# A hybrid streaming encoder on one core: other step sizes for the state-space scans, and ninety matmuls fewer at the end

## The chip, the cores and the metric

The kernel runs on one core of a Trainium2 chip. The metric is the device time of one execution in microseconds (us). TensorE is called PE below, its weight load PEld, VectorE DVE, ScalarE ACT, GpSimd POOL and SyncE SP.

## What is computed

One inference step of an encoder with two layers, for 512 new prompt frames and 64 sample frames, width 1024. Layer one mixes by an S5 state-space recurrence, layer two by differential attention over shared keys and values. Both have a SwiGLU feed-forward block before and after the mixer, and a LayerNorm behind each. All in fp32. The part that the change touches is the recurrence:

```python
bu_re = bu_re.at[:, 0].add(lb_re * h_re - lb_im * h_im)
bu_im = bu_im.at[:, 0].add(lb_re * h_im + lb_im * h_re)
_, _, hs_re, hs_im = lax.associative_scan(complex_affine_combine, (a_r, a_i, bu_re, bu_im), axis=1)
y_blk = jnp.einsum('gcp,btgp->btgc', c_re, hs_re) - jnp.einsum('gcp,btgp->btgc', c_im, hs_im)
```

It is an exact regrouping of a linear recurrence, h(t) = lambda h(t-1) + B u(t), with complex lambda.

## The kernel before, in words

The 576 frames are worked on in two halves: half 0 has 256 columns, half 1 has 320. The weights are cut into tiles of 128 output channels by 7 or 8 rows of 128 inputs. SP loads tile n (`raw`, four buffers), ACT casts it to its high part (`wh`, L509), DVE subtracts that from it for the low part (`wl`, L515), and PE makes three matmuls for each row of it (L537 to L539). There are three buffers of `wh` and `wl`, so the cast of tile n+3 waits until PE is through with tile n (`tile_done`), then comes `wl`, and PE may start tile n+3. DVE also takes the products out of PSUM: L675 (`hf`) in the first product of a feed-forward block, L698 (`r`) in the second.

All engines run programs in order, written out by hand. Work that goes beside the weight tiles is a Python generator; behind each weight tile the code calls `step(beside)`, which issues the work up to the next `yield`. What stands between two `yield`s therefore stands between two `wl` subtractions in DVE's queue. The same count of steps is kept on PE, ACT and POOL, so that the parts meet.

The S5 scans are such side work. `dve_scan` (L1519 on) runs once per half `h` and group `grp` of channels, four times in all: half 0 beside the feed-forward block of half 1, half 1 beside the first block of the next stage, which works on half 0. A scan goes up `LEVELS` = 4 levels and down again. Each call of `advance` is five DVE operations: L1533 (`sa`, a product over m elements a partition), L1535 and L1537 (`sb`, two products of m/2), L1539 and L1542 or L1544 (two additions of m into `hs`). `link` makes the next operation wait for the one before. For half 0 m is 1024, 512, 256 and 128 on the way up, for half 1 it is 1280, 640, 320 and 160; then three or four short calls (m = 32, and 64 in half 1), a few copies, and the levels in reverse order.

`packed(work, room)` divides a scan into steps: each operation yields a size, and a step ends once the sizes have come to `room` (the excess is carried on). The size of an operation is its m plus 60. `SCAN_ROOM` is 1800 for half 0 and 1620 for half 1. `paced(..., SCAN[h])` gives a scan 11 steps in half 0 and 15 in half 1. By these sizes the division (the copies counted as one operation) in half 0 has 3, 2, 3, 4, 10, 17, 7, 5, 2, 2 and 1 operations in its steps, in half 1 it has 2, 2, 1, 2, 3, 5, 10, 17, 7, 4, 3, 1, 2, 2 and 0.

When a scan has ended (its last addition, L1544, raises `s_sh`), PE takes its states in matmuls with the output tables (L1728 and L1731 in `pe_s5`). In PE's program these stand at a fixed step: two steps behind the scan's last one, by the same count. DVE and ACT then copy the results (`ysb`, L1496), ACT takes their gelu (L1653).

At the very end the last rows of the result are transposed (L2529), normalised on DVE (L2569, L2575) and stored by SP (L2591); SP then waits for the stores to land. Behind its last transpose PE has 90 more matmuls (L2923, the loop over `FILL`), which write a PSUM bank that nobody reads.

Of the kernel before, what the change touches and what calls it, by code (L numbers as in the profile page):

```python
# [15 lines left out]
P = 128  # L16
# [72 lines left out]
def _ffn(f, h, held=False):  # L89

    for p in range(len(PARTS)):
# [37 lines left out]
BUSY_TILES = {FIRST["in", 3, 1, 0]: 5}  # L129
BUSY_ROWS = {FIRST["in", 1, 0, 0]: 4, FIRST["o", 1]: 8}  # L130
BUSY_NORMS = {(0, 1): 10, (2, 1): 5, (3, 1): 4}
FILL = ((256, 0, 0), (320, 0, 0), (288, 0, 0), (512, 0, 0), (384, 0, 0), (320, 32, 0), (288, 32, 0), (320, 4, 0), (304, 0, 0),
        (320, 0, 16), (320, 16, 0), (448, 0, 0), (256, 32, 0), (320, 0, 4), (272, 0, 0), (320, 0, 32), (192, 0, 0), (320, 8, 0))

HID = {}
for _f in range(4):
# [94 lines left out]
def build(nc, x_prompt, x_sample, cache_k, cache_v, state_re, state_im, ln_g, ln_b, w_in, w_out,  # L231
# [4 lines left out]
    with ctx:  # L236
# [4 lines left out]
        start = (nc.sbuf_base + 31) // 32 * 32  # L241
# [26 lines left out]
        wh = [keep(f"wh{s}", [P, KMAX, P], F32R) for s in range(WS)]  # L268
# [16 lines left out]
        hh = keep("hh", [P, KMAX, NMAX], F32R)  # L285
        hl = keep("hl", [P, KMAX, NMAX], F32R)
# [115 lines left out]
        ps = ctx.enter_context(nc.psum_tensor("tile_ps", [P, PSS, 512], F32))  # L402
# [51 lines left out]
        def link(eng, ins):  # L454
            steps[0] += 1
            ins.then_inc(step_, 1)
            eng.wait_ge(step_, steps[0])
# [1061 lines left out]
        def dve_scan(dve, h, grp):  # L1519


            V, G = nc.vector, NGRP[h]
            X = hs[:, grp].rearrange("p g i r q -> p g i (r q)")
            halves = (slice(0, GB), slice(GB, 2 * GB))
            dve.wait_ge(s_wc, 2 * (DT * h + 4 * grp + 4))

            def advance(cur, nxt, k, g, n, done=None):

                m = 2 * GB * g * n
                t0, t1 = (t[h][:, 0:m].rearrange("p (g n r) -> p g n r", r=2 * GB, g=g) for t in (sa, sb2))  # L1530
                lre, lim = (lamp[k][:, grp, i].rearrange("p r q -> p (r q)").unsqueeze(1).unsqueeze(1)
                            .broadcast_to([P, g, n, 2 * GB]) for i in range(2))
                V.tensor_tensor(t0, cur, lre, ALU.mult)  # L1533
                yield m + 60
                V.tensor_tensor(t1[..., halves[0]], cur[..., halves[1]], lim[..., halves[0]], ALU.mult)  # L1535
                yield m // 2 + 60
                link(dve, V.tensor_tensor(t1[..., halves[1]], cur[..., halves[0]], lim[..., halves[1]], ALU.mult))  # L1537
                yield m // 2 + 60
                link(dve, V.tensor_tensor(nxt, nxt, t0, ALU.add))  # L1539
                yield m + 60  # L1540
                if done is None:
                    link(dve, V.tensor_tensor(nxt, nxt, t1, ALU.add))  # L1542
                else:
                    V.tensor_tensor(nxt, nxt, t1, ALU.add).then_inc(done, 1)  # L1544
                yield m + 60

            if h == 0:
                link(dve, V.memset(X[:, 0, 0, :], 0.0))
            else:
                V.tensor_copy(X[:, 0, 0, :], carry[:, grp].rearrange("p r q -> p (r q)"))  # L1550
                for ri in range(2):
                    ins = V.tensor_copy(X[:, G - 1, 0, halves[ri]], vs[:, 3 + ri, GB * grp:GB * grp + GB])
                link(dve, ins)
            for k in range(LEVELS):
                s = 1 << k
                yield from advance(X[:, 0:G, s:GB + 1 - s:2 * s], X[:, 0:G, 2 * s:GB + 1:2 * s], k, G, GB // (2 * s))
            end = slice(GB, GB + 1)
            if h:
                yield from advance(X[:, 0:G:G - 1, 0:1], X[:, 0:G:G - 1, end], LEVELS, 2, 1)
            for g in range(1, 4):  # L1560
                yield from advance(X[:, g - 1:g, end], X[:, g:g + 1, end], LEVELS, 1, 1)
            link(dve, V.tensor_copy(X[:, 1:4, 0, :], X[:, 0:3, GB, :]))
            if h == 0:
                V.tensor_copy(carry[:, grp].rearrange("p r q -> p (r q)"), X[:, 3, GB, :]).then_inc(s_carry, 1)
            else:
                for seg in range(2):
                    for ri in range(2):
                        V.tensor_copy(hlast[:, ri, seg, GB * grp:GB * grp + GB], X[:, 3 + seg, GB, halves[ri]]
                                      ).then_inc(s_fin, 1)
            yield 300  # L1570
            for k in range(LEVELS - 1, -1, -1):
                s = 1 << k
                yield from advance(X[:, 0:G, 0:GB + 1 - 2 * s:2 * s], X[:, 0:G, s:GB + 1 - s:2 * s], k, G,
                                   GB // (2 * s), done=None if k else s_sh)
# [20 lines left out]
                                  chained(idle(outputs_at(h, 0) + 4), dve_y(dve, h, 0)),  # L1595
                                  chained(idle(outputs_at(h, 1) + 4), dve_y(dve, h, 1))), s5_steps(h))

        SCAN_ROOM = (1800, 1620)

        def act_u4(act, h):  # L1600
            tables_stored(act)
# [1253 lines left out]
        @block.tensor  # L2855
        def _(pe):

            def ffn(f, h, beside=None, held=False):
                for p in range(len(PARTS)):
                    pe_in(pe, f, h, p, beside)  # L2860
                    if p + 1 < len(PARTS):
                        pe_head(pe, f, h, p + 1, beside)
                    if not (held and p == len(PARTS) - 1):
                        pe_out(pe, f, h, p, beside)
            pe_setup(pe)
            beside = together(pe_rest(pe), chained(idle(START + PARAMS), pe_tables(pe)), chained(idle(SECOND), pe_second(pe)),
                              chained(idle(LN0), pe_ln(pe, 0, 0), pe_s5(pe, 0)))
            ffn(0, 0, beside)
            ffn(0, 1, beside, held=True)
            finish(beside)  # L2870
            pe_plain(pe, ("glu", 0), 0, 2 * DT, X_GELU)
            beside = pe_ln_quick(pe, 1, 0, glu_z, DT)
            pe_out(pe, 0, 1, 2, beside)
            finish(beside)
            beside = chained(pe_ln(pe, 0, 1), pe_s5(pe, 1))
            ffn(1, 0, beside)
            finish(beside)
            beside = pe_ln(pe, 2, 0)
            pe_plain(pe, ("glu", 1), 1, 2 * DT, X_GELU, beside)
            finish(beside)  # L2880
            beside = pe_ln(pe, 1, 1)
            pe_plain(pe, ("v", 0), 0, NH, X_LN2, beside)
            pe_plain(pe, ("k", 0), 0, NH, X_LN2, beside)
            finish(beside)
            beside = pe_kv_rows(pe)
            ffn(1, 1, beside)
            finish(beside)
            beside = chained(pe_ln(pe, 2, 1), idle(1), pe_cached(pe))
            ffn(2, 0, beside)
            finish(beside)  # L2890
            beside = together(pe_ln(pe, 3, 0), chained(idle(9), pe_k_rows(pe)))
            pe_plain(pe, ("k", 1), 1, NH, X_LN2, beside)
            pe_in(pe, 2, 1, 0, beside)
            finish(beside)
            pe_plain(pe, ("q", 0), 0, NH, X_LN3)
            beside = pe_attn(pe, 0)
            pe_out(pe, 2, 1, 0, beside)
            pe_in(pe, 2, 1, 1, beside)
            pe_head(pe, 2, 1, 2, beside)
            pe_out(pe, 2, 1, 1, beside)  # L2900
            pe_in(pe, 2, 1, 2, beside)
            pe_out(pe, 2, 1, 2, beside)
            finish(beside)
            beside = together(pe_ln(pe, 3, 1), chained(idle(LN4), pe_ln(pe, 4, 0)), chained(idle(17), pe_v_rows(pe)))
            pe_plain(pe, ("o", 0), 0, DT, X_ATT, beside)
            pe_plain(pe, ("v", 1), 1, NH, X_LN2, beside)
            pe_plain(pe, ("q", 1), 1, NH, X_LN3, beside, (hh, hl))
            finish(beside)
            beside = pe_attn(pe, 1)
            ffn(3, 0, beside, held=True)  # L2910
            finish(beside)
            pe_plain(pe, ("o", 1), 1, DT, X_ATT)
            n = FIRST["o", 1] + DT - 1
            beside = pe_ln_quick(pe, 4, 1, drained[n % PSS], n // PSS + 1)
            pe_out(pe, 3, 0, 2, beside)
            finish(beside)
            beside = together(chained(pe_ln(pe, 5, 0), pe_y_a(pe)), chained(idle(Y_LAST + 2), pe_y_b(pe)))
            ffn(3, 1, beside)
            finish(beside)
            for cols, at, w_at in FILL:  # L2920
                for j in range(5):
                    w, x = wh[j % 2][:].rearrange("p k c -> p (k c)"), (hh, hl)[j % 2][:].rearrange("p k n -> p (k n)")
                    nc.tensor.matmul(ps[:, 0, 0:cols], w[:, w_at:w_at + P], x[:, at:at + cols],  # L2923
                                     start=True, stop=True, skip_group_check=True)


def rope_tables():
# [38 lines left out]
```

## Time and profile before

| | us |
|---|---|
| median of 3 runs | 2319.38 |
| lowest and highest | 2318.09, 2323.73 |
| the profiled execution: its own time | 2318.73 |
| its span, from the first to the last instruction | 2316.9 |
| PE busy | 2257.6 (97%) |
| DVE busy | 1525.1 (66%) |
| ACT busy | 1144.4 (49%) |
| POOL busy | 575.2 (25%) |

The mean granted TensorE clock was 0.996 of full speed. A time of the trace counts from the first instruction. Matmuls are pipelined: they overlap, so their durations are longer than the distance of their starts. The idle time in square brackets in a timeline is the time for which the engine had nothing to do before this instruction, and behind the arrow stands what ended it. Scans of half 0 lie between 334 and 431 us, those of half 1 between 647 and 762 us.

### The profile page before, as it was taken

The page shows a single profiled execution, that of the slowest core. Times are in us where ns is not written, and L with a number is a line of the kernel's source. Part 1 is how long each engine was busy: PE and PEld are TensorE (multiplying, and loading weights), DVE is VectorE, ACT ScalarE, POOL GpSimd, SP SyncE. Part 2 cuts the span into 40 slices and gives each one's busy share as a digit, 9 for nine tenths or more (in the row PEclk, how much of TensorE's full clock was granted, in tenths as well). Part 3 has the DMA queues.
Part 4 walks back from the last instruction along what each step waited for, and adds up shares of the span by engine and source line. Part 5 has one row for each costly group of instructions (what it writes and reads, how often), then busy time and mean ns, then how long its engine had stood idle before and what let it go on. Part 6 is the DMA issues. An engine that isn't in the chain of part 4 may idle for free.

```text
span 2316.9 us, 42849 instructions
## 1 busy us (share of the span) xinstructions
PE 2257.6 (97%) x17261; PEld 2217.1 (96%) x17261; DVE 1525.1 (66%) x2292; ACT 1144.4 (49%) x1923; POOL 575.2 (25%) x491
## 2 busy tenths in 40 slices
PE   8989999999998998999999999999999999999999
PEld 8989999999998998999999999999999998999999
DVE  6898768657788578444475575656677665475444
ACT  4434543555645546433365465555466564354332
POOL 2267401123211343111251123010352011132110
PEclk9999999999999999999999999999999999999999
DMA  9568675454765455655569656544556456355452
GB/s 251 168 194 234 191 217 181 123 171 137 218 216 172 138 162 148 183 151 147 151 191 291 189 160 178 154 122 134 148 154 189 135 147 190 115 152 170 143 156 80
DMA packets 705367, 391.15 MB, mean 169 GB/s; under 512 B 25001, under 2 KB 693138, under 8 KB 705170
## 3 DMA queue, kind: packets, MB, share of 16 engines
q1 hardware_dynamic: 662720, 332.44, 49.6%
q10 hardware_dynamic: 42450, 55.96, 7.3%
q8 instruction: 138, 2.26, 0.4%
q14 instruction: 59, 0.48, 0.1%
HBM read 366.53 MB, written 21.82 MB: 168 GB/s over the span
## 4 chain that ended last, share of the span: by engine, by line
PE 75%; DVE 9%; ACT 2%; issue 2%; POOL 1%; ACTq 0%; POOLq 0%; DVEq 0%
PE tile_ps L537 22%; PE tile_ps L539 22%; PE tile_ps L538 22%; DVE wl L515 3%; PE misc L1731 1%; PE misc L1711 1%; ACT wh L509 1%; PE misc L2064 1%; PE misc L2089 1%; POOL zq L870 1%; PE misc L2264 1%; DVE r L828 1%; DVE hs L1539 1%; PE tile_ps L2923 1%; PE misc L1728 1%
## 5 line engine op out<-in xcount | busy, mean ns | idle before, releaser
L515 DVE TENSOR_TENSOR wl<-raw,wh 128x1024 fp32r<-128x1024 f32 (+1 forms) x640 | 796.6, 1245 | 444.2 <-ACT wh L509 442.3
L537 PE MATMUL tile_ps<-xh,wh 128*128 128x256 f32 (+1 forms) x3520 | 1051.9, 299 | 21.4 <-DVE wl L515 16.9
L539 PE MATMUL tile_ps<-xh,wl 128*128 128x256 f32 (+1 forms) x3520 | 1035.5, 294 | 0.0
L538 PE MATMUL tile_ps<-xl,wh 128*128 128x256 f32 (+1 forms) x3520 | 1035.4, 294 | 0.0
L509 ACT CAST wh<-raw 128x1024 fp32r<-128x1024 f32 (+1 forms) x640 | 655.0, 1025 | 734.0 <-PE tile_ps L539 723.3
L537 PEld LDWEIGHTS tile_ps<-xh,wh 128*128 128x128 f32 x3520 | 666.1, 189 | 29.5 <-issue 18.7
L538 PEld LDWEIGHTS tile_ps<-xl,wh 128*128 128x128 f32 x3520 | 666.1, 189 | 0.9
L539 PEld LDWEIGHTS tile_ps<-xh,wl 128*128 128x128 f32 x3520 | 665.9, 189 | 0.0
L725 POOL TENSOR_TENSOR hl<-hf,hh 128x256 fp32r<-128x256 f32 (+1 forms) x176 | 243.7, 1384 | 1269.8 <-ACT hh L633 1269.2
L537 PE MATMUL tile_ps<-hh,wh 128*128 128x320 f32 (+1 forms) x1472 | 441.9, 300 | 5.4 <-DVE wl L515 5.1
L538 PE MATMUL tile_ps<-hl,wh 128*128 128x320 f32 (+1 forms) x1472 | 433.0, 294 | 0.0
L539 PE MATMUL tile_ps<-hh,wl 128*128 128x320 f32 (+1 forms) x1472 | 432.8, 294 | 0.0
L537 PEld LDWEIGHTS tile_ps<-hh,wh 128*128 128x128 f32 x1472 | 276.9, 188 | 9.5 <-issue 7.5
L538 PEld LDWEIGHTS tile_ps<-hl,wh 128*128 128x128 f32 x1472 | 277.0, 188 | 0.3
L539 PEld LDWEIGHTS tile_ps<-hh,wl 128*128 128x128 f32 x1472 | 276.8, 188 | 0.0
L698 DVE SCALAR_TENSOR_TENSOR r<-r,tile_ps 128x256 f32<-128x256 f32 (+1 forms) x208 | 94.0, 452 | 142.8 <-PE tile_ps L539 141.5
L627 ACT ACTIVATE sil<-tile_ps 128x320 f32<-128x320 f32 (+1 forms) x140 | 57.6, 412 | 179.6 <-PE tile_ps L539 177.8
L675 DVE SCALAR_TENSOR_TENSOR hf<-sil,tile_ps 128x256 f32<-128x256 f32 (+1 forms) x176 | 79.4, 451 | 79.3 <-PE tile_ps L539 77.0
L633 ACT CAST hh<-hf 128x256 fp32r<-128x256 f32 (+1 forms) x176 | 75.7, 430 | 69.8 <-DVE hf L675 68.2
L764 POOL TENSOR_TENSOR zc<-zc,r 128x256 f32<-128x256 f32 (+1 forms) x64 | 65.3, 1020 | 123.3 <-DVE r L698 76.5
L890 POOL TENSOR_TENSOR xl<-r,xh 128x256 fp32r<-128x256 f32 (+1 forms) x60 | 68.8, 1165 | 91.3 <-ACT xh L803 52.6
L870 POOL TENSOR_TENSOR zq<-zq,sq 128x256 f32<-128x256 f32 (+1 forms) x54 | 61.7, 1142 | 17.5 <-ACT sq L798 11.6
(303 smaller groups left out, 1803.4 us busy)
## 6 DMA issues: line engine op xcount, KB each, us to landing
raw<-in_ffn_w_in_dram SPq DMA_DIRECT2D x352, 512.0 KB, 3.8
raw<-in_ffn_w_out_dram SPq DMA_DIRECT2D x128, 448.0 KB, 3.7
raw<-in_ffn_w_out_dram SPq DMA_DIRECT2D x64, 512.0 KB, 4.0
raw<-in_ssm_w_glu_dram SPq DMA_DIRECT2D x32, 512.0 KB, 3.8
raw<-in_attn_w_kv_dram SPq DMA_DIRECT2D x32, 512.0 KB, 4.0
wt<-scr_w ACTq DMA_DIRECT2D x16, 512.0 KB, 4.7
cp<-scr_c ACTq DMA_DIRECT2D x16, 512.0 KB, 4.3
raw<-in_attn_w_q_dram SPq DMA_DIRECT2D x16, 512.0 KB, 3.9
```

The source lines that it names most:

```text
L509: nc.scalar.copy(wh[n % WS][:, 0:k, :], raw[n % RAWS][:, 0:k, :]).then_inc(w_hi, 1)
L515: nc.vector.tensor_tensor(wl[n % WS][:, 0:k, :], raw[n % RAWS][:, 0:k, :], wh[n % WS][:, 0:k, :].bitcast(F32), ALU.subtract).then_inc(w_lo, 1)
L537: nc.tensor.matmul(o, wh[w][:, kk, :], xa, start=kk == 0, stop=False)
L538: nc.tensor.matmul(o, wh[w][:, kk, :], xb, start=False, stop=False)
L539: return nc.tensor.matmul(o, wl[w][:, kk, :], xa, start=False, stop=kk == ROWS[n] - 1)
L633: nc.scalar.copy(hh[:, i, 0:N], hf[:, 0:N]).then_inc(hh_ready, 1)
L675: nc.vector.scalar_tensor_tensor(out=hf[:, 0:N], in0=sil[:, 0:N], scalar=0.25 if (f, h, p) in TANH else 0.5, in1=bank(n + 1, h), op0=ALU.m ...
L698: nc.vector.scalar_tensor_tensor(out=r[:, d, CS[h]], in0=r[:, d, CS[h]], scalar=alpha, in1=bank(n, h), op0=ALU.mult, op1=ALU.add).then_inc ...
L725: nc.gpsimd.tensor_tensor(hl[:, i, 0:N], hf[:, 0:N], hh[:, i, 0:N].bitcast(F32), ALU.subtract).then_inc(hl_ready, 1)
L764: nc.gpsimd.tensor_tensor(zc[:, 0:N], zc[:, 0:N], r[:, d, CS[h]], ALU.add).then_inc(ln_zc, 1)
L870: nc.gpsimd.tensor_tensor(zq[:, 0:N], zq[:, 0:N], sq[d % 3][:, 0:N], ALU.add).then_inc(ln_zq, 1)
L890: nc.gpsimd.tensor_tensor(low[:, d, 0:NT[h]], r[:, d, CS[h]], high[:, d, 0:NT[h]].bitcast(F32), ALU.subtract).then_inc(x_ready[h], 1)
```

## The change

An operation's fixed part counts 150 in place of 60, the copies in the middle of a scan count four of it in half 1 (600) or two in half 0 (300) in place of 300, and the rooms become 2210 and 1970. The operations, their order and the number of steps (11 and 15) remain. The steps now hold 3, 2, 4, 5, 9, 12, 8, 5, 4, 3 and 1 operations in half 0, and 2, 2, 2, 3, 3, 6, 9, 11, 7, 5, 4, 3, 1, 2 and 1 in half 1. The 90 matmuls at the end of PE's program go.

```diff
-FILL = ((256, 0, 0), (320, 0, 0), (288, 0, 0), (512, 0, 0), (384, 0, 0), (320, 32, 0), (288, 32, 0), (320, 4, 0), (304, 0, 0),
-        (320, 0, 16), (320, 16, 0), (448, 0, 0), (256, 32, 0), (320, 0, 4), (272, 0, 0), (320, 0, 32), (192, 0, 0), (320, 8, 0))
...
                 V.tensor_tensor(t0, cur, lre, ALU.mult)
-                yield m + 60
+                yield m + OP
                 V.tensor_tensor(t1[..., halves[0]], cur[..., halves[1]], lim[..., halves[0]], ALU.mult)
-                yield m // 2 + 60
+                yield m // 2 + OP
                 link(dve, V.tensor_tensor(t1[..., halves[1]], cur[..., halves[0]], lim[..., halves[1]], ALU.mult))
-                yield m // 2 + 60
+                yield m // 2 + OP
                 link(dve, V.tensor_tensor(nxt, nxt, t0, ALU.add))
-                yield m + 60
+                yield m + OP
...
-                yield m + 60
+                yield m + OP
...
-            yield 300
+            yield 4 * OP if h else 2 * OP
...
-        SCAN_ROOM = (1800, 1620)
+        OP = 150
+        SCAN_ROOM = (2210, 1970)
...
-            for cols, at, w_at in FILL:
-                for j in range(5):
-                    w, x = wh[j % 2][:].rearrange("p k c -> p (k c)"), (hh, hl)[j % 2][:].rearrange("p k n -> p (k n)")
-                    nc.tensor.matmul(ps[:, 0, 0:cols], w[:, w_at:w_at + P], x[:, at:at + cols],
-                                     start=True, stop=True, skip_group_check=True)
```

## Rows read from the trace of the kernel before

**Rows 1.** The page: its span, from the first to the last instruction

```profile
span 2316.9 us, 42849 instructions
```

**Rows 2.** Who waited for whom, PE, 330 to 440 us: total, times, longest

```profile
PE tile_ps L537 <- DVE wl L515: 2.0, 2, 1.4
```

**Rows 3.** The same, PE, 640 to 775 us

```profile
PE tile_ps L537 <- DVE wl L515: 8.1, 7, 2.7
PE misc L1728 <- DVE hs L1544: 1.0, 2, 0.6
```

**Rows 4.** Timeline of PE: start, us, engine, line, op [idle before <-releaser]

```profile
431.07 0.43 PE L1728 MATMUL misc<-u,tt 128*128 128x64 f32 x2 [1.68 <-DVE hs L1544]
...
737.66 0.36 PE L537 MATMUL tile_ps<-xh,wh 128*128 128x256 f32 x1 [2.67 <-DVE wl L515]
...
750.89 0.35 PE L537 MATMUL tile_ps<-xh,wh 128*128 128x256 f32 x1 [1.97 <-DVE wl L515]
...
761.75 0.45 PE L1728 MATMUL misc<-u,tt 128*128 128x80 f32 x2 [0.39 <-DVE hs L1544]
```

**Rows 5.** Windows: stretch, its length, busy time (and instructions) of each engine, PEclk

```profile
407.00:431.00 24.00, 20.39 (x136) 19.66 (x135) 23.18 (x51) 17.03 (x25) 4.28 (x3) 1.00 0.45 135
...
722.00:762.00 40.00, 32.59 (x247) 31.55 (x247) 38.53 (x75) 25.89 (x36) 9.86 (x7) 0.91 0.47 139
```

**Rows 6.** The chain that ended last, 718 to 766 us: start, us, what

```profile
743.49 1.05 ACT wh L509
```

**Rows 7.** Timeline of DVE, 345 to 420 us: half 0, groups 0 and 1

```profile
345.04 1.23 DVE L515 TENSOR_TENSOR wl<-raw,wh 128x1024 fp32r<-128x1024 f32 x1 [0.67 <-ACT wh L509]
...
407.44 0.17 DVE L1537 TENSOR_TENSOR sb<-hs,lam 128x16 f32<-128x16 f32 x1
...
418.00 0.42 DVE L1537 TENSOR_TENSOR sb<-hs,lam 128x256 f32<-128x256 f32 x1
...
419.90 0.62 DVE L1496 COPY ysb<-misc 32x256 f32<-32x256 f32 x1
```

**Rows 8.** Timeline of DVE, 659 to 664 us: half 1, group 0

```profile
659.21 0.42 DVE L675 SCALAR_TENSOR_TENSOR hf<-sil,tile_ps 128x256 f32<-128x256 f32 x1 [0.26 <-PE tile_ps L539]
660.35 1.23 DVE L515 TENSOR_TENSOR wl<-raw,wh 128x1024 fp32r<-128x1024 f32 x1 [0.71 <-ACT wh L509]
661.49 1.02 DVE L1537 TENSOR_TENSOR sb<-hs,lam 128x320 f32<-128x320 f32 x1
...
663.40 0.82 DVE L1542 TENSOR_TENSOR hs<-hs,sb 128x640 f32<-128x640 f32 x1
```

**Rows 9.** Timeline of DVE, 722 to 762 us: half 1, group 1

```profile
722.27 1.09 DVE L515 TENSOR_TENSOR wl<-raw,wh 128x896 fp32r<-128x896 f32 x1 [0.54 <-ACT wh L509]
723.28 0.48 DVE L1533 TENSOR_TENSOR sa<-hs,lam 128x320 f32<-128x320 f32 x1
...
723.91 0.32 DVE L1537 TENSOR_TENSOR sb<-hs,lam 128x160 f32<-128x160 f32 x1
...
733.87 0.19 DVE L1539 TENSOR_TENSOR hs<-hs,sa 128x32 f32<-128x32 f32 x1
...
735.22 0.71 DVE L1496 COPY ysb<-misc 32x320 f32<-32x320 f32 x1
...
761.61 1.22 DVE L515 TENSOR_TENSOR wl<-raw,wh 128x1024 fp32r<-128x1024 f32 x1
```

**Rows 10.** Windows of PE alone: stretch, its length, busy time, PEclk

```profile
734.90:738.30 3.40, 0.73 (x6) 1.00 0.04 14
738.30:741.70 3.40, 3.40 (x18) 0.50 0.56 154
```

**Rows 11.** The chain that ended last, its last piece

```profile
2302.33 13.25 PE tile_ps L2923 x90
```

**Rows 12.** Timeline of SP's queue, its last DMA issue

```profile
2313.42 0.52 SPq L2591 DMA_DIRECT2D out_dram<-yrow  x1
```

**Rows 13.** DMA issues, 2300 to 2318 us: size, median us to landing

```profile
out_dram<-yrow SPq DMA_DIRECT2D x1, 256.0 KB, 2.9
```

## The prediction

> **What bounds the kernel now.** The page and its table of busy times come first: PE is busy for 97% of a span of 2316.9 us [rows 1]. An edit that gives PE no less work can only win what PE waits. So the second view is who waited for whom, on PE alone and in the two stretches with scans. In the first, PE waits 2.0 us for `wl` and 1.68 us for the end of a scan [rows 2, 4]. In the second it is 8.1 us and 1.0 us [rows 3]. That is 12.8 us. The third view, the windows of PE around its longest wait, adds something: behind 2.67 us of waiting the granted clock is 0.50 for 3.4 us, the lower of its two levels, 1.2 GHz [rows 4, 10]. The clock cost 1.7 us of PE work there. It fell again behind the wait of 1.97 us at 751 us, which is why the mean clock from 722 to 762 us is 0.91 [rows 4, 5]; I count that fall as equally long. The most that any division of the scans can win is 12.8 + 3.4 = 16.2 us, 0.7%.
>
> The fourth view is how full DVE is where PE waits: 23.18 of 24 us before the scan of half 0 ends, 38.53 of 40 us before the last of half 1 ends [rows 5]. There DVE is the bound, and PE meets it again where it needs the end of the scan (L1728). What counts is not when each `wl` comes but when DVE is through with everything queued in front of the scan's last addition.
>
> **The scans, part by part.** The change moves no operation in the scan's own order. It moves the points at which `wl`, `hf`, `r` and `ysb` stand among the operations. DVE's total work stays. The end of a scan moves by three things only: scan work done earlier, in front of DVE's last idle time; idle time that this work fills or that a new wait makes; and work of other kinds that now stands in front of the last addition.
>
> Half 0, group 0. PE's only waits of this stretch for `wl` are two, and both come later [rows 2]. The new steps 2 and 3 put 0.7 to 0.8 us more in front of a `wl`. DVE is ahead there: it idles 0.67 us before the `wl` at 345.04 until the cast comes, and the cast waits for PE [rows 7]. So the added work meets idle time. Bounds 0 and 0.8 us, taken 0, since PE has no wait there at all.
>
> Half 0, group 1. DVE's chain is unbroken from 407 us. The fourth step ends one operation later (L1537, whose place is up to 0.2 us [rows 7]), in front of that point. The last two steps end where they did. So the end of the scan comes 0.2 us earlier. On the way, the new step 7 leaves out three operations that stood in front of a `wl`: from 418.00 to 419.90, 1.9 us [rows 7]. So the 1.4 us wait at 422 goes [rows 2] and PE comes to the scan's end sooner, but it can't pass it. The three waits of 3.7 us become about 1.1 and 2.3 us, together 3.5 us. Gain 0.2 us.
>
> Half 1, group 0. DVE's last idle times are 0.26 and 0.71 us, at 659 and 660 us [rows 8]. By the new division two operations more stand in front of them, which took from 661.49 to 663.40, 1.91 us; 0.5 us of this was a stretched first one, so I take 1.4 us. They fill the idle time and push the `wl` at 660.35 by 0.3 us. Net 1.1 us sooner. Against this, the last step was empty and now holds the last addition, so that one more `wl` stands in front of it, here of 896 columns, 1.0 us (1.09 for one of this size [rows 9], of which some overlaps). Gain 0.1 us. PE waits for one `wl` less and at the scan's end 1.5 us in place of 0.6.
>
> Half 1, group 1. DVE's chain is unbroken from 722.27 on. The new division has two operations more in front of this point: 723.28 to 723.91, 0.63 us [rows 9]. One `wl` moves in front of the last addition, 1.1 us (the one at 761.61 takes 1.22 and overlaps a little with its successor [rows 9]). And one wait grows: the `wh` cast at 743.49 follows ACT's chain from the fourth `ysb` copy, not DVE's room [rows 6]. The copy comes 2.0 us sooner, since the new step 7 has four operations fewer at its end, 733.87 to 735.22 = 1.35 us [rows 9], on top of the 0.63. DVE itself would be there 2.3 us sooner, so it waits 0.3 us. The sum is -0.6 + 1.1 + 0.3 = 0.8 us later. Bounds: -0.6 us if the moved `wl` falls into idle time, and 2.8 us (-0.6 + 1.1 + 2.3) if the cast comes no sooner than before. The new step 11, three operations in place of one, delays one `wl` against its neighbours, but nothing at the end.
>
> **The clock.** Longer single waits can cost what the division does not. Here the clock fell behind waits of 2.67 and 1.97 us and did not behind 1.68 us [rows 4, 10]. I expect about 2.3 us at the end of half 0, 1.5 us at the first scan end of half 1, and in the last stretch about 0.9, 1.3, 1.4, 0.7, 2.0, 2.5 and 2.0 us. A fall inside the last stretch is paid out of PE's waits, as the two falls there now are. A fall right behind the end of half 0 or of the last scan is paid in full: 1.7 us each. Two places, each a little better than even for the first and below even for the second: one fall is the likeliest. Bounds 0 and 5.1 us (three scan ends, 1.7 us each); I take 1.7 us.
>
> **The matmuls at the end.** The chain of the page ends in them, 13.25 us from 2302.33 [rows 11]. They look like the end of the kernel, but they are through at 2315.6. SP issues its last store at 2313.42, and that one takes 2.9 us to land [rows 12, 13], so until 2316.3, and behind it come SP's own waits and the last barrier, to 2316.9 [rows 1]. The store's landing hides the end of the matmuls by 0.7 us. Nothing else of PE, and no DMA, waits behind them. When they go, the store is still last. Effect 0. From below it is bounded by the 0.6 us from the landing to the end of the span, if PE's part of the last barrier took all of that; from above by 0, as nothing is added.
>
> **The sum.** -0.2 (half 0) - 0.1 (half 1, group 0) + 0.8 (group 1) + 0 (end) + 1.7 (one fall of the clock) = +2.2 us. Against the profiled execution of 2318.73 us this gives 2320.9 us. That execution is 0.65 us below the median of 2319.38; with it the forecast is 2321.5 us.
>
> **Rivals.** First, no fall of the clock on the path: +0.5 us, 2319.9 us. For it speaks that waits up to 1.68 us cost none, and that my two waits of 2.0 to 2.3 us are worked out, not measured. By the Trainium skill, page "TensorE: Matmul & The Clock Gate", only idle gaps longer than any that I expect are to be avoided mid-kernel; by that rule this rival would be the outcome, but the fall behind 1.97 us in this trace speaks against it. Second, two or three falls: 2323.2 to 2324.9 us. Third, the unevenness is what costs, and the waits of PE go with it: the whole 16.2 us would give 2303 us, and half of it 2311 us. It needs a DVE that has room in front of the scan ends; 96% of busy time there [rows 5] speaks against it. Fourth, on the other side, slower beyond doubt: the `wl` moved in front of the last addition, at both scan ends of half 1, unpaid by any idle time (+1.1 and +1.0 us), ACT's late cast (+0.3 us), and falls of the clock behind all three ends and behind one more wait (+6.8 us) give 9.2 us, 2328.6 us. It decides only from four paid falls on. Fifth, the change doesn't do what it says: the steps were meant to be even, and where DVE has no idle time their evenness decides nothing. If then the clock stays as it is, the time is that of the first rival less or more 0.5 us: no difference. I count it with the first.
>
> **How the numbers follow.** One fall 0.42, none 0.31, two or three 0.15, waits gone 0.05, slower beyond doubt 0.07. A measurement of this kernel can tell about 0.3% from no change, 7 us. The first three cases all lie within it (2312.4 to 2326.3 us): 0.88. Faster 0.05, slower 0.07. The range is 2316.5 to 2326.9 us. Its low end is the rival without a fall, 2319.9 us, less the 3.4 us of the two falls that are there now, should they go and count after all. Its high end is three falls, 2324.9 us, with the upper bound of the last group (2.0 us above what I took).
>
> **What would show it.** PE's 1.4 us wait at 422 us is gone, and its wait at L1728 about 431 us is near 2.3 us in place of 1.68. At 699 us it is near 1.5 us, at 762 us near 2 us. DVE is busy for the same time over each scan. The last addition of both groups of half 1 stands behind one more `wl`. The wait of 2.67 us near 738 us is below 1.5 us. The span ends with the last store, 0.6 us behind its landing, and PE's last instruction is at 2302 us. I am wrong if PE's waits over both stretches sum to less than 10 us with the clock at 1.00 throughout, or if the clock falls in stretches where no scan runs and the kernel before had no fall.

## The result, and the profile after

The changed kernel takes 2327.51 us (median of 7 runs, 2325.68 to 2331.45) against 2320.38 us (7 runs, 2317.69 to 2323.73): a ratio of 1.0034, 95% interval 1.0023 to 1.0045. It is 7.1 us slower, just beyond the high end of the forecast range, 2326.9 us. The profiled execution has a span of 2325.7 us, 8.8 us more than before.

PE's waits in the two stretches with scans, 330 to 440 us and 640 to 780 us (releaser, us in total, times, longest); they answer to [rows 2, 3]:

```profile
PE misc L1727 <- DVE hs L1542: 2.7, 1, 2.7
PE tile_ps L535 <- DVE wl L513: 1.6, 1, 1.6
```

```profile
PE tile_ps L535 <- DVE wl L513: 10.0, 7, 2.8
PE misc L1727 <- DVE hs L1542: 2.7, 2, 2.2
```

(The lines of the changed kernel lie one or two lower.) The waits at the scan ends grew as forecast, from 1.7 to 2.7 us and from 0.6 to 2.2 us. The timeline of PE has them, to be read beside [rows 4]:

```profile
432.82 0.55 PE L1727 MATMUL misc<-u,tt 128*128 128x64 f32 x2 [2.69 <-DVE hs L1542]
...
704.15 0.45 PE L1727 MATMUL misc<-u,tt 128*128 128x80 f32 x2 [2.16 <-DVE hs L1542]
```

Shortly behind both, the windows of PE show its clock at the lower level (stretch, length, busy time with the count of instructions, granted clock, DMA share and GB/s). Four such windows of 3.4 us follow; the first two lie behind 432.8 us, the third behind 704.2 us, the last in the crowded stretch of half 1:

```profile
432.90:436.30 3.40, 3.40 (x17) 0.52 0.56 162
436.40:439.80 3.40, 3.40 (x15) 0.50 0.85 249
706.10:709.50 3.40, 3.40 (x18) 0.50 0.49 136
760.70:764.10 3.40, 2.81 (x13) 0.50 0.51 145
```

In the kernel before, no fall stood on the path in these places; its two falls there were inside the crowded stretch [rows 5, 10]. Where the span's 8.8 us come from can be read from the starts of `wl`, of which the n-th is the same in both kernels:

| from the `wl` at, to the `wl` at (us, kernel before) | changed kernel longer by |
|---|---|
| 8.4 to 359.3 (setup, first scan's beginning) | 0.9 |
| 359.3 to 471.2 (ends of both scans of half 0) | 4.1 |
| 471.2 to 638.1 | -0.8 |
| 638.1 to 722.3 (half 1, group 0) | 2.3 |
| 722.3 to 793.3 (half 1, group 1) | 0.7 |
| 793.3 to 1682.5 | -0.1 |
| 1682.5 to 2292.0 | 1.7 |

The first and the last entry hold falls of the clock in parts that the change doesn't touch: at 84.8 and 142.9 us and at 1767.6 us. The four entries from 359.3 to 793.3 us come to 6.3 us.

The end of the kernel goes as told. The last pieces of the chain are now DVE's, and the matmuls are gone from it; SP's last of three stores follows:

```profile
2319.65 1.20 DVE yrow L2568
2320.88 1.28 DVE yrow L2574
```

### The profile page after: what moved, and what is told of

The parts are those of the page before. It is cut to its first block, busy times and chain, and to the rows that moved or that the text cites. A ratio compares the mean times of both kernels' runs of the same rounds, so it can differ in the third digit from the quotient of the medians.

```text
span 2325.7 us, 42671 instructions
## 1 busy us (share of the span) xinstructions
PE 2247.5 (97%) x17171; PEld 2207.1 (95%) x17171; DVE 1525.6 (66%) x2292; ACT 1144.1 (49%) x1923; POOL 574.4 (25%) x491
## 4 chain that ended last, share of the span: by engine, by line
PE 75%; DVE 9%; ACT 2%; issue 2%; POOL 2%; ACTq 0%; POOLq 0%; DVEq 0%
PE tile_ps L535 22%; PE tile_ps L536 22%; PE tile_ps L537 22%; DVE wl L513 3%; PE misc L1730 2%; PE misc L1710 1%; POOL zq L868 1%; ACT wh L507 1%; PE misc L2063 1%; PE misc L2088 1%; PE misc L2263 1%; PE misc L1727 1%; DVE r L826 1%; DVE hs L1537 1%; PE misc L2241 0%
```

## The experiments

All ran with the kernel before beside them on the same chip (its medians: 2320.54, 2320.86 and 2320.11 us in the three groups). Times are medians; a ratio is to the kernel before, with its 95% interval.

### Which part costs it

e1: only the matmuls at the end go.

```diff
-            for cols, at, w_at in FILL:
-                for j in range(5):
-                    ...
```

> Only the 90 matmuls at the end of TensorE's program are gone; the scans keep their old steps. Theory (the scans' steps cost the 7 us, through longer waits at the scan ends and falls of the clock behind them): the same as before, within 0.5 us of 2320.4 us, since the last store lands behind the matmuls. Rival A (the missing matmuls cost it, by what they do to the clock near the end or to the next execution): 3 to 7 us slower, 2324 to 2327 us.

Measured: 2320.2 us, 0.9995 (0.9986 to 1.0004). Its trace is one microsecond longer than that of the kernel before and has the same falls, and one more behind PE's last work, which nothing waits for. The matmuls were hidden, as the forecast had it, and rival A is out.

e2: only the scans' steps change, the matmuls stay.

> Only the scans' steps are the new ones; the 90 matmuls at the end stay. Theory: all of the change's time, 2327 to 2328 us, with TensorE's waits at the ends of the scans as in the changed kernel (2.7 us near 433, 2.2 us near 704) and the clock at half behind them. Rival A: most of the loss is absent, 2320 to 2323 us.

Measured: 2331.3 us (5 runs), 1.0040 (1.0026 to 1.0054), 3 us above what was expected. The scans are all of the change. The waits at 433 and 702 us are 2.69 and 2.16 us, as expected, but the falls are only in part where they were told: one of 3.4 us at 435.6 us, none behind 702 us, and one of 6.8 us at 766.7 us, behind the last scan end.

```profile
765.64 0.45 PE L1729 MATMUL misc<-u,tt 128*128 128x80 f32 x2 [1.69 <-DVE hs L1544]
```

```profile
702.40:706.40 4.00, 4.00 (x32) 1.00 0.76 215
766.70:773.50 6.80, 6.80 (x34) 0.50 0.51 152
```

e3 and e4 use the new sizes in one half only.

```diff
-                yield m + 60
+                yield m + OP[h]
-            yield 300
+            yield MID[h]
-        SCAN_ROOM = (1800, 1620)
+        OP, MID = (150, 60), (300, 300)       # e3; e4: (60, 150), (300, 600)
+        SCAN_ROOM = (2210, 1620)              # e4: (1800, 1970)
```

> The new sizes and room in the scans of half 0 alone; half 1 and the 90 matmuls as before. Theory: the wait at the scan end near 431 us grows from 1.7 to 2.5 or 2.7 us, and the clock falls behind it for one or two periods of 3.4 us, each paid with 1.7 us: 2 to 4 us slower, 2322 to 2324 us. Rival B (only the half 1 division counts, where one more weight subtraction stands in front of the last addition): no change, 2320.4 us.

> The new sizes and room in the scans of half 1 alone. Theory: the last addition stands behind one more weight subtraction in both groups; with this the ends come about 0.8 us later, and the clock falls on the path behind the first and behind the last: 0.8 to 4.2 us slower, 2321 to 2325 us. With half 0 alone it adds up to the whole. Rival B: all of the 7 us, 2327 us.

Measured: e3 2325.3 us, 1.0017 (1.0008 to 1.0026); e4 2325.7 us, 1.0018 (1.0010 to 1.0027). Each half costs 4 to 5 us (by the ratios and by the medians), and they add up to the whole. Both medians lie above what was expected before these runs, by 1.3 and 0.7 us. Rival B is out both ways. The forecast for half 0 alone had been a small gain and perhaps one fall; e3's trace has a wait of 2.69 us at 431.8 and a fall at 434.1 us, e4's a wait of 1.97 us at 700.1 and a fall of twice 3.4 us at 700.7 us.

e3's trace tells one thing more. Its half 1 has the old steps, but the clock stayed up through it, though its longest wait was as long as in the kernel before:

```profile
700.80 0.45 PE L1729 MATMUL misc<-u,tt 128*128 128x80 f32 x2 [0.61 <-DVE hs L1544]
...
739.31 0.36 PE L537 MATMUL tile_ps<-xh,wh 128*128 128x256 f32 x1 [2.60 <-DVE wl L515]
...
763.40 0.45 PE L1729 MATMUL misc<-u,tt 128*128 128x80 f32 x2 [0.41 <-DVE hs L1544]
```

```profile
722.00:764.00 42.00, 32.06 (x265) 1.00 0.48 141
```

From the first scan end of half 1 to the last it took 62.60 us, with no fall, and 62.60 us in the kernel before, with two. There the last end is in [rows 4] and the first is this:

```profile
699.15 0.45 PE L1728 MATMUL misc<-u,tt 128*128 128x80 f32 x2 [0.61 <-DVE hs L1544]
```

So the two falls of the kernel before cost nothing. Without them PE's waits for `wl` there come to 10.6 us in place of 8.1: a sum of waits depends on how many falls the trace happened to catch.

### Is it the clock, or the later scan ends?

e5 and e9 leave the scans as in the changed kernel and fill PE's wait at two scan ends with matmuls that nobody reads. PE then has less idle time, and the scan ends at the same instant.

```diff
+        SCAN_BUSY = {(0, 1): 18, (1, 0): 14}      # e9: 10 and 8
...
-                pe.wait_ge(s_sh, 2 * h + grp + 1)
                 pe.wait_ge(s_wc, 2 * DT * (h + 1))
...
+                pe_busy(misc[:, 0, 0:P], SCAN_BUSY.get((h, grp), 0))
+                pe.wait_ge(s_sh, 2 * h + grp + 1)
```

> The changed kernel, and in it TensorE fills most of its wait at two scan ends with matmuls that nobody reads: 18 at the end of half 0, 14 at the first scan end of half 1. The scans and the instants at which they end stay. Theory (the clock's falls behind these waits are most of the loss): no fall near 433 and near 706 us, 3.4 to 5 us less than the changed kernel, 2322 to 2324 us. Rival (only the later scan ends cost time, the falls are a by-product): 2327 to 2328 us as in the changed kernel, or more if the matmuls come out longer than the waits.

Measured: 2325.6 us, 1.0022 (1.0013 to 1.0031). Neither theory's time. No fall is at the two scan ends. The timeline of PE shows one reason for the loss: the matmuls outlast the wait. The scan ended at 432.1 us, the tables' matmuls could start only at 433.31.

```profile
429.29 4.18 PE L524 MATMUL misc<-vec,ones 128*128 128x128 f32 x36
433.31 0.33 PE L1729 MATMUL misc<-u,tt 128*128 128x64 f32 x2
```

So the count was wrong (one such fp32 matmul is two instructions in the trace and takes 0.23 us), and e9 mends it. The other reason is a fall of 6.8 us at 765.7 us, behind a wait of 2.12 us at the last scan end, which had no matmuls.

> As e5_busy, with 10 and 8 matmuls in place of 18 and 14. In e5_busy they ran 4.2 and 3.3 us and outlasted the waits by about 1.2 and 0.9 us. Theory (falls behind the waits): 2.3 and 1.8 us of matmuls fit into the waits of 2.7 and 2.2 us; no fall near 433 and 704 us, 2 us less than e5_busy, 2323 to 2324.5 us. Rival (the later ends alone cost it): 2327 to 2328 us as in the changed kernel.

Measured: 2322.98 us, 1.0012 (1.0003 to 1.0020). In its timeline of PE the matmuls fit, a short wait is left at both ends, and in its windows the clock stays at 1.00 behind both:

```profile
429.40 2.39 PE L524 MATMUL misc<-vec,ones 128*128 128x128 f32 x20
432.26 0.43 PE L1729 MATMUL misc<-u,tt 128*128 128x64 f32 x2 [0.47 <-DVE hs L1543]
...
698.15 1.95 PE L524 MATMUL misc<-vec,ones 128*128 128x128 f32 x16
700.48 0.45 PE L1729 MATMUL misc<-u,tt 128*128 128x80 f32 x2 [0.38 <-DVE hs L1543]
```

```profile
432.00:436.00 4.00, 3.74 (x31) 1.00 0.60 174
436.00:440.00 4.00, 4.00 (x34) 1.00 0.72 211
...
704.00:708.00 4.00, 4.00 (x36) 1.00 0.46 140
```

The scans take as long as in the changed kernel: from the same `wl` to the scan end 24.98 and 39.35 us, against 24.96 and 39.36. They cost 2.9 us (2322.98 - 2320.11) in place of 7.1 us, or of the 10.3 us that the changed kernel lost in the same group (e12), once PE is kept busy in front of two of their ends. Added work made the kernel faster. So the larger part of the loss, some 4 to 7 us, is the clock behind these two waits.

The traces price a single fall, since those of the changed kernel, e2, e6, e9 and e12 have the same scans in half 0, and all but e6's in half 1. They differ in how long the clock was low behind a scan end (e4 has the same scans in half 1 alone, e3 in half 0 alone). By the starts of `wl`, longer than the kernel before by:

| stretch (us, kernel before) | no fall | 3.4 us low | 6.8 us low | 10.2 us low |
|---|---|---|---|---|
| 359.3 to 471.2, end of half 0 | 0.9 (e9) | 2.4, 2.5, 2.5 (e12, e2, e3) | 4.1 (changed) | 5.6 (e6) |
| 638.1 to 722.3, first end of half 1 | 0.8, 0.8 (e9, e2) | 2.3, 2.4 (changed, e12) | 3.8 (e4) | |
| 722.3 to 793.3, last end | 0.7, 0.7, 0.8 (changed, e12, e9) | | 3.8 (e2) | |

Each 3.4 us at the lower level cost 1.4 to 1.7 us, and the scans by themselves 0.7 to 0.9 us in each stretch. In e5 the overlong matmuls cost 1.1 and 0.7 us against e9, the fall at the last end 2.9 us.

The traced execution of e12 is one of its two fastest. That the others lost more to the clock is in the granted clock of all executions: the mean of e12's six is 0.9890, of e9's eleven 0.9921. That is 7 us of PE at full speed (25.6 against 18.3 us lost), and the two medians differ by 7.4 us.

### What stands in front of the last addition

e6: the changed kernel, but in half 1 the last two additions share a step, so no `wl` stands between them.

```diff
                 link(dve, V.tensor_tensor(nxt, nxt, t0, ALU.add))
-                yield m + OP
+                yield 0 if h and done is not None else m + OP
```

> The changed kernel, but in half 1 the last addition of a scan joins the step in front of it, so no weight subtraction stands between the last two additions; all other steps as in the changed kernel. Theory: the scan ends of half 1 come 1.0 to 1.1 us sooner, TensorE's wait near 704 us is 1.1 us in place of 2.2, and the fall behind it goes: 1 to 4 us less than the changed kernel, 2323.5 to 2326.5 us. Rival (the weight subtraction in front costs nothing, since TensorE waits for it next anyway): 2327 to 2328 us.

Measured: 2325.6 us, 1.0019 (1.0010 to 1.0028). The wait near 704 us is 0.97 us in place of 2.16, and no fall is behind it. A fall of 10.2 us, from 432.3 us on, stands behind the end of half 0, which has the wait of the changed kernel, 2.68 us. From the `wl` at which DVE last waited in the kernel before to the end of the scan it takes 38.35 us in e6, in the changed kernel 39.36 us: the moved `wl` costs 1.0 us, as forecast. The timeline of DVE in e6 has the two additions in one piece and both `wl` behind them:

```profile
700.77 1.91 DVE L1537 TENSOR_TENSOR hs<-hs,sa 128x1280 f32<-128x1280 f32 x1
702.72 1.49 DVE L1542 TENSOR_TENSOR hs<-hs,sb 128x1280 f32<-128x1280 f32 x1
704.13 2.09 DVE L513 TENSOR_TENSOR wl<-raw,wh 128x896 fp32r<-128x896 f32 x2
```

e7 and e8 go the other way from even steps: larger rooms, so that scans take more of DVE's free time at their beginning and leave the last steps empty.

```diff
-        SCAN_ROOM = (2210, 1970)
+        SCAN_ROOM = (2600, 2450)       # e7; e8: (2450, 2200)
```

> The changed kernel with rooms of 2600 and 2450 in place of 2210 and 1970: the scans fill 9 of 11 and 12 of 15 steps, and the last steps are empty. Theory (idle time of VectorE before the crowded stretch decides, with what stands in front of the last addition): 1.7 to 3 us more work is done in front of the crowded stretches, waits at the scan ends vanish with the falls behind them, and what is left is waits for weight subtractions: 5 to 12 us less than the changed kernel, 2316 to 2322 us. Rival (even steps over all 11 and 15 are best): the larger steps delay more weight subtractions, 2328 us or more.

> As the one with rooms of 2600 and 2450, with rooms of 2450 and 2200: 10 of 11 and 13 of 15 steps. Theory: about half of its gain, 2319 to 2325 us. Rival: 2327 us or more.

Measured: e7 2324.2 us, 1.0019 (1.0010 to 1.0027); e8 2319.7 us, 0.9993 (0.9984 to 1.0001). The wait at the scan ends is gone in both, but e7 misses its forecast. Its `wl` waits between 640 and 780 us come to 12.8 us, but e8's to 11.6 us, so that is at most a small part of the reason. e7's trace has a fall in front of the end of half 0, which e8's hasn't, behind a wait for `wl`:

```profile
426.80 0.39 PE L535 MATMUL tile_ps<-hh,wh 128*128 128x320 f32 x1 [1.96 <-DVE wl L513]
```

The clock fell at 427.5 us. From 359.3 to 471.2 us e7 takes 1.2 us more than the kernel before, e8 0.6 us less. Over all executions the mean granted clock is 0.9908 in e7 and 0.9931 in e8, about 5 us of PE at full speed, and the medians differ by 4.5 us. In e8, PE's waits in the two stretches are these:

```profile
PE tile_ps L535 <- DVE wl L513: 2.8, 2, 1.5
```

```profile
PE tile_ps L535 <- DVE wl L513: 11.6, 9, 2.0
```

That is 14.4 us, more than the 12.8 us of the kernel before, but in pieces of at most 2.0 us and with fewer falls: behind 230 us only at 741.9 and 905.8 us, and none at a scan end. So fewer waits in total is not what makes e8 as fast as the kernel before.

e10: room 2450 and size 150 in half 0 alone, half 1 as before (with `OP[h]` and `MID[h]` as in e3).

```diff
-        SCAN_ROOM = (1800, 1620)
+        OP, MID = (150, 60), (300, 300)
+        SCAN_ROOM = (2450, 1620)
```

> The kernel before, with sizes of 150 and a room of 2450 in the scans of half 0 alone, which then fill 10 of 11 steps. Theory: the end of the second scan of half 0 comes sooner and TensorE's wait for it goes, while half 1 keeps its empty last step: 0.5 to 2 us less than the kernel before, 2319 to 2320.5 us. Rival (the old division is the best for both halves): 2321 us or more.

Measured: 2318.9 us, 0.9994 (0.9986 to 1.0003). Its median is the lowest of all, 1.2 us under the kernel before, but the interval holds 1. Nothing here beats both kernels beyond doubt; e8 and e10 beat the changed one by about 8 us or more.

### Falls far behind the scans

e11: the kernel before with 3 us of unread matmuls in front of a weight tile behind all scans.

```diff
-BUSY_TILES = {FIRST["in", 3, 1, 0]: 5}
+BUSY_TILES = {FIRST["in", 3, 1, 0]: 5, FIRST["glu", 1]: 13}
```

> The kernel before with 13 matmuls that nobody reads in front of the first weight tile of the second gated product, behind all scans: they push everything behind them by 3.0 us and touch no scan. Theory of knock-on falls (a wait of 2.2 us near 1760 us, the same in every kernel, meets a fall of the clock in each traced kernel that comes there 3 us or more later than the kernel before, and not in the kernel before): more than 3.0 us slower, 4.5 to 6 us, 2325 to 2327 us, with a fall near 1765 us. Rival: 3.0 us and no fall there, 2323.9 us.

Measured: 2323.3 us, 1.0009 (1.0001 to 1.0018), 3.2 us above the kernel before. By the time the rival holds, but by luck. In the trace the matmuls run for 3.06 us at 809.8 us and make the stretch from 793.3 to 1682.5 us longer by only 0.85 us, as part of them stands in place of a wait: the kernel before waits 1.5 us at 814 us, e11 doesn't. Another 1.1 us came in the setup. So the wait near 1760 us came 1.4 us later, not 3. And the trace does show a fall near 1763 us, with which the last stretch is 1.8 us longer:

```profile
1763.10:1766.50 3.40, 3.40 (x18) 0.50 1.15 347
```

e10's trace has a fall at 1759.6 us as well, and its wait there ends at 1758.3 us, 2.0 us sooner than in the kernel before. So what decides on a fall near 1760 us isn't lateness. Of 14 traces of this study, 11 have one there, those of the kernel before, e1 and e8 do not. The stretch from 1682.5 to 2292.0 us is 1.5 to 2.0 us longer in the 11 than in the kernel before, 0.1 and 0.2 us in e8 and e1. The fall comes with the old steps too (e11) and with the new sizes it can be missing (e8), so I count it as none of the change's; what sets it stays open.

e12: the changed kernel again.

> The changed kernel once more, beside the others on the same chip. Both theories: 2327 to 2329 us. It tells from a second trace which falls belong to it: theory, falls behind the scan ends near 433 and 704 us again; rival, falls at random places with none behind the scan ends.

Measured: 2330.4 us (6 runs), 1.0042 (1.0029 to 1.0055). Its waits at the two scan ends are 2.68 and 1.97 us, and the falls are there again, the first 2.5 us behind the scan end and only once 3.4 us long. The median lies above the 2327 to 2329 us that were expected, that of the first seven runs within.

```profile
435.30:438.70 3.40, 3.40 (x15) 0.50 0.75 215
705.00:708.40 3.40, 3.40 (x18) 0.50 0.49 130
```

## Why the prediction was wrong, step by step

**What bounds the kernel: right.** DVE is the bound in the crowded stretches, and making the steps even didn't take PE's waits away; they came to 17.0 us after 12.8. Part of this growth is only that the crowded stretch caught one fall in place of two, and e3 shows that falls there swallow waits. The third rival, waits gone, is out, by e2 to e4.

**Half 0: the sign was wrong, the waits nearly right.** The wait at 422 us went, 1.6 us came at 427 us where 1.1 was told, and 2.69 us at the scan end where 2.3 was told. But from the `wl` at 406.43 us to the end of the scan it took 24.58 us before and 24.96 us after (from 407.80): 0.4 us later, not 0.2 sooner. The timeline of DVE in the changed kernel shows where:

```profile
427.91 1.65 DVE L1537 TENSOR_TENSOR hs<-hs,sa 128x1024 f32<-128x1024 f32 x1
429.59 0.49 DVE L696 SCALAR_TENSOR_TENSOR r<-r,tile_ps 128x320 f32<-128x320 f32 x1
429.99 1.11 DVE L513 TENSOR_TENSOR wl<-raw,wh 128x896 fp32r<-128x896 f32 x1
431.02 1.74 DVE L1542 TENSOR_TENSOR hs<-hs,sb 128x1024 f32<-128x1024 f32 x1
```

The first addition took 1.65 us, where the same one took 1.23 us before. POOL's `xl` operations began 0.46 us before it, in the kernel before 0.15 us behind its start; whether they stretched it was not tested. Group 0 was put at 0 us, with an upper bound of 0.8: the stretch from the `wl` at 359.34 us to that at 406.43 us came out 0.5 us longer. Against this, 471.2 to 638.1 us came out 0.8 us shorter, which the sum doesn't have; it varies among the traces, and its cause stays open.

**Half 1, group 0: the term was mis-sized.** From the `wl` at 660.35 us to the end of the scan it took 38.75 us before and 39.36 us after. I had told +0.3 us for that `wl` and in sum -0.1 us, and had counted DVE's last idle time at 660 us. In the changed kernel DVE idles again behind it, twice, for ACT's cast:

```profile
671.95 1.22 DVE L513 TENSOR_TENSOR wl<-raw,wh 128x1024 fp32r<-128x1024 f32 x1 [0.41 <-ACT wh L507]
...
679.39 1.23 DVE L513 TENSOR_TENSOR wl<-raw,wh 128x1024 fp32r<-128x1024 f32 x1 [0.42 <-ACT wh L507]
```

In front of each wait DVE had come through a step sooner than before, and the cast had not. Behind the `wl` at 664.74 us three smaller operations stand, 3.17 us to the next `wl` in place of 3.91 us, and the wait is at the `wl` behind that one. The second wait is behind the step that holds 11 small operations in place of 17. The prediction has such a wait in group 1 only.

**Half 1, group 1: the scan right, the waits not.** From the `wl` at 722.27 us to the end of the scan 39.43 us before, 40.05 us after, so 0.6 us later; told was 0.8. Of the last three waits told, 2.0, 2.5 and at the scan end 2.0 us, the first two came as 1.82 and 2.84 us, the third as 0.55 us. In the changed kernel and in e12 (0.44 us) a fall just in front of it stands in its place; in e2 and e5, without that fall, it was 1.69 and 2.12 us. In the timeline of DVE the moved `wl` stands between the last two additions, here in group 0:

```profile
701.61 1.09 DVE L513 TENSOR_TENSOR wl<-raw,wh 128x896 fp32r<-128x896 f32 x1
702.62 1.48 DVE L1542 TENSOR_TENSOR hs<-hs,sb 128x1280 f32<-128x1280 f32 x1
```

Together the scan ends come 1.6 us later (0.4 + 0.6 + 0.6), where +0.5 us was told. By the stretches of the first table, less the falls, it is 1.6 us as well (6.3 - 4.7).

**The clock: right mechanism, wrong count, and this made the prediction wrong.** I took one paid fall, 1.7 us, and gave two or three a chance of 0.15. The changed kernel's trace has 6.8 us at the lower level behind 432.8 us and 3.4 us behind 704.2 us, thus three times 3.4 us. Against the traces without a fall there they cost 3.2 and 1.5 us, 4.7 us together. e9 gives 4 to 7 us as the clock's part, over its 11 runs. The failed step is this term of the sum, 1.7 us where 4.7 were measured, and behind it the scans' terms, +0.5 us where 1.6 were measured. Together they are 6.3 us of the measured 7.1 us. The fourth rival, which needed four paid falls, was closest to the time, but not by these parts.

Two premises of the term failed. A fall was taken as 3.4 us long, and behind a scan end it can be twice that, in e6 three times. And I had taken the first scan end of half 1 as safe, at a forecast wait of 1.5 us, close to the 1.68 us that cost nothing; the idle DVE above made it 2.16 us. Both rested on four waits in two stretches. Outside them, the trace of the kernel before speaks against a limit between 1.68 and 1.97 us: the clock fell at 229.7 us behind a wait of 1.74 us, and did not behind 2.64 and 2.22 us. It also has a fall of 6.8 us, at 123.9 us.

```profile
229.22 0.69 PE L1387 MATMUL misc<-cp,ebuf 128*32 128x128 f32 x16 [1.74 <-POOL cp L1372]
906.71 0.36 PE L537 MATMUL tile_ps<-xh,wh 128*128 128x256 f32 x1 [2.64 <-DVE wl L515]
1760.30 0.89 PE L2064 MATMUL misc<-kT,qT 64*128 64x256 f32 x7 [2.22 <-ACT ex L2144]
```

```profile
123.90:130.70 6.80, 6.24 (x28) 0.50 0.38 114
229.70:233.10 3.40, 3.40 (x31) 0.50 0.97 288
906.70:910.10 3.40, 2.98 (x24) 1.00 0.54 157
1760.30:1763.70 3.40, 3.40 (x32) 1.00 1.13 346
```

One of the prediction's signs of being wrong came too: the clock fell where no scan runs and the kernel before had no fall, at 84.8, 142.9, 924.5 and 1767.6 us. But e11, with the old steps, has a fall at 1763.1 us, and e10 one at 141.7 us, in front of all scans, so the sign tells little of the change.

What all traces together bear is a chance, not a limit. At the end of half 0 a fall stands behind 2.7 us of waiting in five of five traces and behind 1.7 us in none of four. At the first end of half 1 it stands behind 2.0 to 2.2 us in three of four. At the last end it stands behind 1.7 and 2.1 us (e2, e5), 6.8 us long both times, and behind none of the shorter waits.

By the Trainium skill, page "TensorE: Matmul & The Clock Gate", section "Why this matters for your kernels", only idle gaps longer than these are to be avoided mid-kernel. These traces do not bear that out: the clock was at half behind waits of 2.69 and 2.16 us, and e9 shows the gain from filling them. The measurement decides.

**The matmuls at the end: right.** e1 shows no difference.

## What to carry to other kernels

Side work that is cut into even steps gains nothing where its engine is full anyway: add up what stands in front of the instant for which the bounding engine waits, and look for new idle time in every step that becomes shorter. A longer single wait can cost more than its length, as the clock may fall behind it: in half 0 the wait at the scan end grew by 1.0 us, and the falls behind it cost 1.5 to 4.7 us. A fall in front of a place where PE waits anyway costs nothing, so ask of each whether PE is the bound behind it. Don't judge a division by the sum of its waits in one trace, as falls change that sum. Where such a wait can't be shortened, matmuls that nobody reads, sized to end before it, win back most of that (here 18 of them, 4 to 7 us). Sized too long, as in e5, they cost 1.8 us of it, and they do nothing for the scan end that has none.

## What the runs showed of the hardware

The clock fell behind single waits of 1.69 us (e2, at 766 us) and 1.74 us (kernel before, at 229 us) to 2.92 us (e9, at 756 us), on an engine that was 97% busy over the span in the kernel before; a wait of 2.64 us passed without a fall (kernel before, at 907 us). Its low stretches were 3.4 us long or two or three times that (e6: 10.2 us from 432.3 us on). Where PE was the bound, each 3.4 us cost 1.4 to 1.7 us; where PE waited for DVE anyway, two of them cost nothing (kernel before against e3, 62.60 us both). The same kernel showed 6.8 us behind one scan end in one execution and 3.4 us in another. Falls in stretches with the same work came and went from trace to trace, near 85, 143, 920 and 1765 us, which is some of why single runs of one kernel differ by up to 8 us: of the kernel before in the last group, the run of 2317.65 us had a mean granted clock of 0.997, those of 2324.34 and 2324.97 us had 0.993.
